# Shift, decay and feature steps of a head-pair loop rewritten and reordered in a two-layer RWKV-7 / Fourier / Conformer / mixture kernel

## The reference, cut to what matters

```python
r = r + (centred_shift(r) - r) * mu_rkv[0]      # the same for k and v
decay = exp(-exp(-softplus(-w_pre) - 0.5))      # = exp(-exp(-0.5) * sigmoid(w_pre))
icl = sigmoid(a0 + ...)
kk = heads(k * k_k); kk = kk / max(norm(kk), 1e-12)
k_dir = heads(k * (1 + (icl - 1) * k_a))
S = S * w_t - (S @ kk_t) (kk_t * a_t)^T + v_t k_t^T          # state of a head, per token
y_t = S r_t
out = (groupnorm(y) + sum(r * k * r_k) * v) * gate
```

## Time and profile before

| | us |
|---|---|
| median of 3 runs (2401.15 to 2403.99) | 2403.42 |
| the profiled execution | 2401.35 |
| its span in the profile | 2399.4 |
| PE busy in the span | 2243.7 (94%) |
| DVE busy | 936.9 (39%) |
| ACT busy | 397.0 (17%) |
| POOL busy | 167.3 (7%) |

### The profile page before, as it was taken

The page is one execution under the profiler, slowest core; times in us unless marked ns, Lnnn a source line. Parts: engine busy times, 40 slices in busy tenths (PEclk is TensorE's granted clock), DMA queues, the critical chain, the costliest instruction groups (busy, mean ns, idle before and its releaser), DMA issues. The chain is left out here.

```text
span 2399.4 us, 56100 instructions
## 1 busy us (share of the span) xinstructions
PE 2243.7 (94%) x23412; PEld 1282.6 (53%) x23412; DVE 936.9 (39%) x1965; ACT 397.0 (17%) x685; POOL 167.3 (7%) x162
## 2 busy tenths in 40 slices
PE   5998989999888889999999999889998999999997
PEld 2446777777676765544444444545555444444444
DVE  2357666676757621211111111479613111111113
ACT  2022323232323201000000000211312000000001
POOL 1001010100101000000000000000000000000000
PEclk8998999999999999999999999899999999999999
DMA  9981010101000035799999999502036999999995
GB/s 369 386 316 32 2 33 2 32 2 32 13 22 21 2 122 197 268 383 393 395 396 393 394 396 390 193 1 70 1 140 255 395 397 394 393 397 393 392 392 172
DMA packets 181670, 538.56 MB, mean 224 GB/s; under 512 B 12545, under 2 KB 54145, under 8 KB 181410
## 3 DMA queue, kind: packets, MB, share of 16 engines
q1 hardware_dynamic: 175202, 515.16, 55.8%
q0 software_dynamic: 6336, 21.63, 3.8%
HBM read 510.81 MB, written 25.95 MB: 224 GB/s over the span
## 5 line engine op out<-in xcount | busy, mean ns | idle before, releaser
L2108 PE MATMUL ps<-raw,xs 128*64 128x512 f32 x3072 | 673.8, 596 | 4.0 <-PEq L2102 3.9
L2108 PEld LDWEIGHTS ps<-raw,xs 128*64 128x64 f32 x3072 | 217.7, 137 | 431.0 <-issue 429.6
L2120 PE MATMUL ps<-raw,xs 128*32 128x256 f32 x6144 | 342.3, 380 | 3.2 <-PEq L2102 3.2
L2120 PEld LDWEIGHTS ps<-raw,xs 128*32 128x32 f32 x6144 | 195.1, 110 | 134.0 <-issue 10.4
L2299 DVE SCALAR_TENSOR_TENSOR h<-h,ps 128x768 f32<-128x768 f32 x32 | 30.5, 954 | 461.9 <-DVEq L2298 461.9
L1644 DVE COPY_PREDICATED wk<-m,ps 128x128 f32<-128x128 uint8 x360 | 101.4, 352 | 116.4 <-DVEq L1640 116.2
L2426 PE MATMUL ps<-h,raw 128*128 128x512 f32 (+1 forms) x448 | 124.7, 440 | 7.2 <-PEq L2417 7.2
L2227 ACT ACTIVATE h<-ps 128x768 f32<-128x768 f32 x32 | 25.9, 811 | 595.1 <-ACTq L2226 595.1
L900 PE MATMUL ps<-h,wk 128*128 128x512 f32 (+1 forms) x416 | 121.4, 438 | 1.5 <-PEq L1216 1.3
L1030 PE MATMUL ps<-wk 64*64 64x64 f32 x2400 | 102.9, 223 | 14.5 <-PEq L1006 13.8
L1044 PE MATMUL ps<-wk 64*64 64x64 f32 x2400 | 98.5, 219 | 5.0 <-PEq L1006 3.2
(11 more groups left out here) (333 smaller groups left out, 2643.9 us busy)
## 6 DMA issues: line engine op xcount, KB each, us to landing
raw<-in_moe_w_gate SPq DMA_DIRECT2D x64, 2048.0 KB, 18.0
raw<-in_moe_w_up SPq DMA_DIRECT2D x64, 2048.0 KB, 20.0
raw<-in_moe_w_down SPq DMA_DIRECT2D x64, 2048.0 KB, 19.1
wk<-in_mod_w SPq DMA_DIRECT2D x24, 2048.0 KB, 12.1
wk<-in_ev_w_in SPq DMA_DIRECT2D x18, 512.0 KB, 5.3
raw<-in_od_w_in SPq DMA_DIRECT2D x4, 2048.0 KB, 15.2
hrow<-rows SPq DMA_DIRECT2D x10, 512.0 KB, 2.9
ysum<-low SPq DMA_DIRECT2D x10, 512.0 KB
```

Source lines behind the costliest of these rows:

```text
L2108: last = pe.matmul(ps[to:to + CAPS, bank_of(kind, ee)], XS[ee][:, c, 0:CAPS], raw[:, slot(l, 2 * m + c // 4), c % 4, 8 * to:8 * to + 512], ...
L2120: last = pe.matmul(ps[to:to + 32, bank_of(kind, ee) + 1, 0:256], XS[ee][:, c, CAPS:], raw[:, slot(l, 2 * m + c // 4), c % 4, 8 * to:8 * to ...
```

## The change: one-operation shifts, folded affine steps, other buffers, another order

- *Shifts.* The row x + (n/2 - x) mu (n the sum of the neighbours) is written as (1 - mu) x + (mu/2) n. ScalarE makes (1 - mu) x in a new step `scale_raw(s)` (Identity with a per-partition scale, SBUF to SBUF, 128x640); VectorE adds the second term in one operation, after waiting for `shf_ready` and the new `raw_scaled`. The tables of per-channel factors in `vectors` get one more small operation.
- *Affine steps folded.* `decay` loses its affine step: the scan now adds the ones (`add, add` instead of `mult, add`), and the factor goes into the scale of `exps`. `key_features` loses its affine step: it goes into the per-channel factors, and `norm_features` uses (t + 1) and -0.5 in the two operations that it had.
- *Buffers.* `place` of the values becomes 0, the keys' buffer, so `copy_raw(VV)` waits for `icl_used` (after `norm_features(1)`). The y copy goes to the queries' raw row and waits for `r_shifted` in place of `ahead_done`.
- *Order, VectorE.* `decay(0)` ahead of `shift(K)`; `key_features(1)` ahead of `advance(1)`; `queries(1)` ahead of `y_centred`.
- *Order, TensorE.* The two small products of the rates are put apart (`low_rank`), the first ahead of the wait for the copy of u(0). The keys' norm product (`knorm`) moves from `ahead(5)` to `ahead(4)`, ahead of s(1); one piece of the queries' projection moves behind s(1).
- *ScalarE.* A tanh of one column (`warm`) stands in the levels loop of pairs with a follower, after the eighth copy; its table load replaces the one before the steps.

```diff
             ysb, yc, ysq, root, gate = proj[:, 0], proj[:, 1], lw0, rkv[:, 1], shf[:, 1]
-            place = (1, 0, 1)
+            ysb, yc, ysq, root, gate = proj[:, 1], proj[:, 0], lw0, rkv[:, 1], shf[:, 1]
+            place = (1, 0, 0)
...
                     FILL = {
-                        1: (lambda: slot_read(),),
-                        2: (lambda: slot_read(), lambda: low_ranks(1, (0, 1))),
+                        1: (lambda: low_rank(1, 0, 0), lambda: slot_read()),
+                        2: (lambda: slot_read(), lambda: low_rank(1, 1, 1)),
                         3: (lambda: slot_read(), lambda: project(Q, 0, (0, 1, 2))),
-                        4: (lambda: project(Q, 0, (3, 4, 5)),),
-                        5: (lambda: slot_read(), lambda: knorm(1), lambda: project(Q, 0, (6, 7))),
+                        4: (lambda: slot_read(), lambda: knorm(1), lambda: project(Q, 0, (3, 4))),
+                        5: (lambda: project(Q, 0, (5, 6, 7)),),
...
                         if s == VV:
-                            act.wait_ge(sem("r_shifted"), 1).then_inc(sem("r_shifted"), -1)
+                            act.wait_ge(sem("icl_used"), 1).then_inc(sem("icl_used"), -1)
...
+                    def scale_raw(s):
+
+                        act.activation(rkv[:, s], proj[:, place[s]], ACT.Identity, scale=hv[:, ONE_MU + s:ONE_MU + s + 1]).then_inc(act_done, 1)
+                        done("raw_scaled")
...
-                        act.activation(eP[:, z], rel[:, z], ACT.Exp).then_inc(act_done, 1)
+                        act.activation(eP[:, z], rel[:, z], ACT.Exp, scale=-EXPH / 2).then_inc(act_done, 1)
...
+                            if following and u == NT + 2:
+                                act.activation(warm, eps[:, 0:1], ACT.Tanh).then_inc(act_done, 1)
...
                         if following:
                             decay_tanh(0, q=2)
+                            scale_raw(K)
...
+                            if following and j == 2:
+                                scale_raw(Q)
...
                                     copy_raw(VV, 0, "win_free")
+                                    scale_raw(VV)
                         if following:
-                            act.wait_ge(sem("ahead_done"), 1).then_inc(sem("ahead_done"), -1)
+                            act.wait_ge(sem("r_shifted"), 1).then_inc(sem("r_shifted"), -1)
...
-                        dve.tensor_scalar(lw[z], lw[z], -EXPH / 2, -EXPH / 2, ALU.mult, ALU.add).then_inc(dve_done, 1)
-                        done()
                         for tt in range(NT):
-                            dve.tensor_tensor_scan(..., 0.0, ALU.mult, ALU.add).then_inc(dve_done, 1)
+                            dve.tensor_tensor_scan(..., 0.0, ALU.add, ALU.add).then_inc(dve_done, 1)
...
-                        dve.scalar_tensor_tensor(out, out, 0.5, src, ALU.mult, ALU.subtract).then_inc(dve_done, 1)
-                        done()
-                        dve.scalar_tensor_tensor(rkv[:, s], out, col("mu", s), src, ALU.mult, ALU.add).then_inc(dve_done, 1)
+                        dve.wait_ge(sem("raw_scaled"), 1).then_inc(sem("raw_scaled"), -1)
+                        dve.scalar_tensor_tensor(rkv[:, s], shf[:, place[s]], hv[:, HALF_MU + s:HALF_MU + s + 1], rkv[:, s], ALU.mult, ALU.add).then_inc(dve_done, 1)
...
-                        dve.tensor_scalar(b, b, 0.5, 0.5, ALU.mult, ALU.add).then_inc(dve_done, 1)
-                        done()
-                        dve.tensor_scalar(kn, b, col("k_a"), hv[:, 16:17], ALU.mult, ALU.add).then_inc(dve_done, 1)
+                        dve.tensor_scalar(kn, b, hv[:, HALF_KA:HALF_KA + 1], hv[:, ONE_KA:ONE_KA + 1], ALU.mult, ALU.add).then_inc(dve_done, 1)
```

More of the change, by code:

```diff
@@ L778, in even_heads @@
             hpv = ca(NHPV)
-            hv = ca(NHPV + 5)
+            hv = ca(NHPV + 13)
+            warm = ca(1)
             gnv = ca(2)
@@ L910, in low_ranks, with low_rank @@
                                     last.then_inc(sem("e_ready"), 1)
+                    def low_rank(s, z, q):
+                        for a, b in halves:
+                            last = pe.matmul(pair(q)[:, a:b], w2[z * HD:z * HD + HD, s], lora[z * HD:z * HD + HD, s, a:b], start=True, stop=True)
+                        last.then_inc(sem("e_ready"), 1)
                     def knorm(q):
@@ L1260, in decay_tanh @@
                         act.wait_ge(sem("e_ready"), 1).then_inc(sem("e_ready"), -1)
-                        act.activation(lw[z], pair(1 - z if q is None else q), ACT.Tanh, scale=0.5, bias=hv[:, 12 + z:13 + z]).then_inc(act_done, 1)
+                        act.activation(lw[z], pair(1 - z if q is None else q), ACT.Tanh, scale=0.5, bias=hv[:, HALF_W0 + z:HALF_W0 + z + 1]).then_inc(act_done, 1)
                         done("e_read", "lw_ready")
@@ L1268, in icl_tanh @@
                             act.wait_ge(sem("k_shifted"), 1).then_inc(sem("k_shifted"), -1)
-                        act.activation(icl[z], pair(q), ACT.Tanh, scale=0.5, bias=hv[:, 14 + z:15 + z]).then_inc(act_done, 1)
+                        act.activation(icl[z], pair(q), ACT.Tanh, scale=0.5, bias=hv[:, HALF_A0 + z:HALF_A0 + z + 1]).then_inc(act_done, 1)
                         done("e_read", "icl_ready", *names)
@@ L1679, in heads @@
                             vectors()
+                            decay(0)
                             shift(K)
-                            decay(0)
                         advance(0)
```

31 lines of the change are left out of this document (18 added, 13 removed).

## The result

The changed kernel took 2381.65 us, median of 4 runs (2381.05 to 2384.46), against 2403.7 of the kernel before beside it: ratio 0.9906, 95% interval 0.9891 to 0.9922. The forecast was 2384, with a range of 2372 to 2394. The profiled execution took 2382.25 (span 2380.3), 19.1 less than that of before; the forecast said 19.0.

What follows compares the result with a forecast made beforehand. No engine is full, so waits decide: VectorE up to 388, TensorE to 411, then VectorE. Five pairs at 3.0 plus 4.0 for the opening make 19.0; 2401.35 becomes 2382.3, median 2.1 above, so 2384, range 2372 to 2394.

Steps and rivals of the forecast that it cites:

- The middle belongs to TensorE: Middle of a pair's steps, 388 to 411 us: TensorE bounds, so VectorE waits about 3 us before advance(2).
- To the first old state: Start of a pair's steps: load gone, shift moved behind; first old state at 387.5, not 388.01.
- The squares' wait: Norm product ahead of s(1) waits for the squares, using up 0.5; s(1) stays at 396.8, second old state at 401.
- Third old state, y's mean, masks: Late in a pair: third old state 1.0 earlier, y's mean 2.0 earlier, masks at 426.6 in place of 429.74.
- The clock: Rival, 15%: TensorE's lower clock in every pair's early steps, each losing 1.5, 7.5 of the 19, so 2392.
- The list of TensorE: In the steps: norm product moved ahead of s(1), which stays at 396.8; small product fills idle time before s(0).
- The opening: Before the first pair's products: VectorE's chain 4.4 earlier, TensorE's list ending 1.1 later; gain 4.0.
- The scan: In each decay: adds keep the scan at 0.40; rival, 4%: 0.83 each, so 2410.
- The load: Levels loop: warm tanh's 1.28 load hidden in a 2.69 gap; by the skill's page, sum 1.5 less.

Runs made afterwards that it cites:

- e2: Changed kernel plus four VectorE operations of 128x640 behind normed_k, ahead of advance(2); 2380.56 us.
- e1: Changed kernel without the warm tanh, so the table load stands before the first decay tanh of the steps again; 2389.99 us.
- e9: Kernel before the change with only the warm tanh added, so the table load lies in the levels loop; 2401.16 us.
- e5: Changed kernel plus four small unused matmuls on TensorE in the idle time before the first old state; 2378.46 us.
- e6: Changed kernel with TensorE's list of work ahead as before the change: norm product late, the two small products of the rates together; 2377.61 us.
- e12: Changed kernel with TensorE's list as before the change and the second key features behind the second increment again; 2381.72 us.
- e7: Changed kernel without the warm tanh, with TensorE's list, second key features and second queries placed as before the change; 2397.05 us.
- e11: Changed kernel with TensorE's old list, keys' shift behind first increment, keys' scaling behind u(0)'s copies, opening's squares ahead of the rates' tanh; 2386.05 us.

## Why the prediction was right, point by point

*The middle belongs to TensorE* held. The wait before advance(2) is 3.00, TensorE has no gap over 0.24 from the first old state to the masks, and e2 filled the wait at no cost.

*To the first old state* the sum was 0.5 and came out at 0.48 (387.53 in place of 388.01). e1 and e9 add that load and shift are one step: taking away the load alone brings the first old state 0.12 earlier (e9), the rest of the change without it puts it 0.79 later (12.22 in e1, 11.43 before), and both together bring 0.48.

*The squares' wait* was seen at 0.24 (0.5 said), s(1) at 396.74 (396.8), the second old state at 400.88 (401).

*Third old state, y's mean, masks:* 1.31, 2.52 and 3.73 earlier for 1.0, 2.0 and 3.1 in the prediction. Each stretch adds 0.1 to 0.3 to what was missed, and the masks of a pair without a fall come 3.7 earlier, not 3.1 (53.16 in the second pair before, 49.43 in the third after). Which part of the change gave the wait before y's mean back was not tried by itself.

*The clock* was a rival at 15% for all pairs, at 1.5 each. It came in three of five, at 1.25 to 1.27 (50.68 and 50.70 against 49.43; the fifth pair's 50.85 has 0.17 from ahead of the fall), and ate, at 0.75 a pair, what the terms had missed: five pairs at 3.7 would have been 18.6, an estimate from the pairs without a fall. So the 15.0 of the forecast and the 15.7 measured in the steps agree by luck, as two errors cancel. In the kernel before, a fall cost only 0.4 (third pair 53.53, second 53.16): it began ahead of the first old state, where TensorE's idle time went from 1.41 to 0.21. In e9, whose falls also begin there, they cost 0.3 to 0.8. Its cause as the prediction has it, the idle time before the first old state (1.9 there, 1.03 measured), did not stand: e5 fell with that time filled; e6 had 1.08 and 1.18 idle in its steps and fell in none of them, and e12, with the same two, fell in four. In thirteen other profiles with and without the change the falls come in none to five of the five pairs. What decides it stays open.

*The list of TensorE* had no gain of its own in the prediction: the early norm product's wait eats the 0.5 won ahead of it, and the small product counts as a help against the clock. e6 undoes both together and loses nothing: undisturbed pairs are 0.25 shorter, about the wait for the squares, so this part of the change cost time. VectorE still waits 1.73 before advance(2), so it did not need the early product.

*The opening* was forecast at 4.0 and gave 2.8 from the start, 4.0 from the keys' projection (first masks 51.98 behind it, before 56.02; the projection itself began 1.2 later in this execution). That the 4.0 was met is luck too: in nine of the ten other runs with this opening the distance is 50.2 to 50.5, a gain of 5.5 to 5.8. In those nine VectorE sets the end: it has no wait for TensorE at the modulation's results (0.44 of idle time), and TensorE waits 1.47 for it in the first products (e1). In the changed kernel's execution TensorE set it, as the prediction has it: VectorE's shift was not held up (0.88 at 189.18, in the nine 2.84), and the clock fell in the queries' projection (10.50 in place of 8.82). The tenth run, e5, is like it. In these two the factors of the first pair arrived just as GpSimd summed the keys' neighbours, and a small operation of `vectors` was held up until the sum ended (VectorE, then GpSimd):

```profile
154.69 0.86 DVE L1479 COPY wk<-wk 128x12 f32<-128x12 f32 x1 [11.02 <-DVEq L1478]
```

```profile
154.28 1.25 POOL L1451 TENSOR_TENSOR x<-x 128x638 f32<-128x638 f32 x1 [9.01 <-POOLq L1450]
```

In e1 that copy took 0.17, ahead of the sum. So the first decay tanh came 11.9 behind the keys' projection (11.7 in e5) and not 10.3 to 10.6, and the norm product 1.1 to 1.6 later than in the nine. The fall followed; that it came of this delay is not shown.

*The scan* took 0.405 for 0.403, so its rival is out; what bounds a scan no run shows.

*The load:* the Trainium skill, "ScalarE: Activation LUTs", section "What ACT_TABLE_LOAD costs", adds a drain of about 1.4 to the load. No run here shows one: e1 pays 1.28 for the load's 1.28, and the warm load hides in 2.68.

## What to carry to other kernels

Time saved on an engine counts only in the stretch where that engine is late: here the operations saved, with the new buffers, gave at most 0.9 a pair (e7, with falls of the clock), and two of the moves, of the load and of the queries, gave 1.3 and 1.2. Two edits can be one step, so undo each part in the changed kernel and also try it alone in the old one; the load was worth 1.28 in the one and 0.12 in the other. Where a disturbance comes and goes between executions, compare marks of undisturbed stretches, not medians, and distrust a sum that fits before its terms do. A wait that is taken away may have hidden something: a fall of the clock cost 0.4 in a pair before and 1.25 after.

## What was not expected of the hardware

A VectorE operation that begins while GpSimd works can be held up: 1.45 in place of 0.49 in e12, and a shift of 2.84 in the opening of e11 and of the nine runs, 0.88 in the changed kernel's, where it ended before GpSimd's copy began (190.06 and 190.87). Not every one is: the masks of 429.74 in the kernel before, which read PSUM, took 0.68 to 0.69 each beside a GpSimd copy of 2.32 (429.70), as elsewhere. The reciprocal took 4.15 in every profile, and GpSimd's sum ran inside it at its usual 1.25 (in e6 from 504.31 to 505.56, beside the reciprocal of 503.93), while a sum that began inside a product of 0.82 took 1.56 (402.41 in the kernel before). The reciprocal began first each time; the other order no run shows. The Trainium skill, "SBUF — State Buffer", section "Terms", has the two engines share a pair of ports under an exclusive lock. e12's row agrees with it in size: the 0.96 over the usual 0.49 is most of the 1.10 that GpSimd's operation still had to run (394.39 to 395.49).

The clock fell amid matmuls without a gap: in e5, 2.8 us behind the last idle time, of 0.48, and at the same place in the fourth pairs of e1 and e2. It fell once for 13.7 us in the steps of one pair (e1's fourth), which cost some 4 against its undisturbed pair.
